# A one-core encoder kernel: attention outputs scaled by turned inverse sums instead of scaled probabilities, exponentials one pair ahead, dots moved behind attention

## The chip, the cores and the metric

The kernel runs on one core of one Trainium2 chip. The metric is the device time of one execution in microseconds. Before the change three runs took 2780.69, 2788.65 and 2793.71 us, so the median is 2788.65 us. Everything is float32.

## What is computed

One layer of a hybrid encoder is applied to two batches of 512 tokens of width 1024, with shared weights. Cut to what matters here:

```
h  = RMSNorm(x);  z = h @ W_in            # pool channels | q | k | v | two gates
A  = pooling mixer(pool channels)
s  = (q . k) * 64**-0.5                   # 8 query heads share 2 key/value heads, head size 64
pr = softmax(s, over 512 keys);  B = pr @ v
x += W_out( sigmoid(gate_pool) * (A @ W_pool_out) + sigmoid(gate_attn) * (B @ W_attn_out) )
# PEER: per token 8 heads x 16 experts = 128 experts out of 16384
a   = h2 . expert_u[idx]                  # 128 dot products of 1024 per token
x  += sum( gelu(a) * softmax gate * expert_v[idx] )
y   = RMSNorm(x)
```

The softmax subtracts the row's maximum, takes exponentials, and divides by their sum over the 512 keys.

## The kernel before

**Groups.** A batch has four tiles of 128 tokens. The mixer runs in three groups (`GROUP_OF`, L65): group 0 is tiles 0 and 1 of batch 0, group 1 its tiles 2 and 3, group 2 all four tiles of batch 1. A group goes through gates and pooling products, attention, eight steps of gate and attention products (`attn_out`), output products in chunks of 256 columns (`out`), the second norm, and the queries and keys of PEER. The order on each of the five engines is written out by hand in one block per engine; semaphores tie them together. Six PSUM banks go round over all jobs of TensorE in the order that `jobs_of` (L172) yields. A job waits until the bank of six jobs ago is freed.

**Attention.** A step is one tile, one pair of heads and one of its halves, so a tile has eight steps, or four pairs. For a pair TensorE does the scores of the next pair (L872, 128x512 into a bank each), the values of the pair before (L886, into `o_banks`), and then the transposes of this pair's probabilities (L703, four of 128x128 a step). VectorE takes each row's negative maximum (L1559). ScalarE takes the exponential with the sum in `prob_sum` (L1175). VectorE inverts the sum (L1566). The probabilities are then multiplied by it: by VectorE in group 0 (L1569), by ScalarE in groups 1 and 2 (L1191). TensorE turns them, and ScalarE moves the two turned banks to SBUF (L1048, into `gate_attn` or `keys_sb`) for the values. At the end of a tile ScalarE moves the outputs from an `o_bank` to `attnT` (L1180).

**Gathered rows.** From the first queries on, GpSimd gathers expert rows from DRAM one slot of 128 tokens at a time (L1429, 128 rows of 4 KB each, here called a row). The order is fixed: 128 rows of `expert_u` of tile (0,0), 128 of `expert_v`, the same for tile (0,1), then three more tiles. A row goes to one of twelve ring slots and may be asked for when the slot's last user is done. VectorE uses a `u` row by one dot product over 1024 columns (L1464, `dot(count)`), and frees the slot. The number of dots at each place of VectorE's program is written by hand:

```
            attention(2, 1)
            softmax(2)
            softmax(3)
            split_ids(0)
            dot(11)
            attn_out(2, (7, 7, 7, 7, 7, 6, 0, 0))
            zero_sums(1)
            turn_ids(2, 1)
            dot(4)
            out(2, (4, 4, 4, 4, 4, 4, 4))
            norm2(2)
```

The numbers in brackets are the dots behind each step. TensorE starts the output products only when all eight merged steps are there (`merged_ready`, L942). What is left of the 128 dots is done early in the queries of group 2; then ScalarE takes the gelu (L1275), VectorE weighs it by the gates (L1843), and TensorE turns the weights (L764). In group 1 the rows of the first tile are used likewise. The last stage, from about 1415 us on, streams all experts once for the three tiles that are done densely, and adds the remaining gathered tiles beside it.

## Time and profile before

| What | us |
|---|---|
| median of three runs | 2788.65 |
| profiled execution | 2784.83 |
| its span | 2783.0 |
| TensorE busy (matmuls) | 2589.6 (93%) |
| VectorE busy | 2035.8 (73%) |
| GpSimd busy | 1556.3 (56%) |
| ScalarE busy | 537.8 (19%) |

The mean granted TensorE clock is 0.972 of full speed. The gathers' queue moves 671.17 of 996.18 MB. The three attention stages lie at 149 to 182, 372 to 408 and 821 to 903 us.

In the rows below, PE is TensorE's matmuls, PEld its weight loads, DVE VectorE, ACT ScalarE, POOL GpSimd. A row of an engine in time has its start, how long it lasted in us, the engine, the source line, and in brackets the idle time just before it with what ended it. "x8" counts instructions as the profiler records them: a float32 matmul appears twice. "issue" and "remote" are idle times without a releaser that the profile knows.

### The profile page before, as it was taken

To read this page: it belongs to the slowest core of one execution; us is meant where nothing else is said; L and a number is where in the kernel's file an instruction comes from. 1 tells how busy PE (TensorE), PEld (TensorE's weight loads), DVE (VectorE), ACT (ScalarE), POOL (GpSimd) and SP (SyncE) were. 2 spreads that over 40 slices of the span, in tenths; PEclk is the share of its full clock that TensorE was granted. 3 is DMA by queue.
4 is the path that set the end of the run, shared out by engine and by line. 5 is a ranking of instruction groups with operands and counts; after the bars stand their busy time and mean duration, and the time that the engine had idled before them with its cause. 6 is when DMAs were issued, how large, how long until landed. Compare 5 with 4: busy or idle time off the path is not lost.

```text
span 2783.0 us, 30841 instructions
## 1 busy us (share of the span) xinstructions
PE 2589.6 (93%) x9957; PEld 1551.2 (56%) x9957; DVE 2035.8 (73%) x4558; ACT 537.8 (19%) x1206; POOL 1556.3 (56%) x1284
## 2 busy tenths in 40 slices
PE   7999989989997998998699999999999999999997
PEld 6867868875334475554554455455545455445553
DVE  1232977877348877788789988977777877877788
ACT  2141151211018014554510000100000000000101
POOL 0000155455665785444277786786777666766674
PEclk9999999989999999999799999999999999999998
DMA  6538789988997898999899999999999999999997
GB/s 239 184 120 299 282 310 406 405 320 312 395 374 254 324 411 319 336 350 333 296 362 413 413 412 413 391 408 413 413 412 413 413 413 413 415 412 413 413 404 285
DMA packets 305988, 996.18 MB, mean 358 GB/s; under 512 B 26432, under 2 KB 107200, under 8 KB 276672
## 3 DMA queue, kind: packets, MB, share of 16 engines
q0 software_dynamic: 184320, 671.17, 62.3%
q1 hardware_dynamic: 69664, 292.02, 26.9%
q10 hardware_dynamic: 51872, 31.46, 3.7%
q8 instruction: 54, 0.88, 0.1%
q14 instruction: 78, 0.64, 0.1%
HBM read 932.68 MB, written 61.87 MB: 357 GB/s over the span
## 4 chain that ended last, share of the span: by engine, by line
PE 34%; DMA 27%; DVE 19%; issue 12%; POOL 3%; ACT 3%; another core or an unknown queue 1%; DVEq 0%; ACTq 0%; POOLq 0%
PE bank L725 13%; DMA ring<-in_expert_v,idx 12%; PE bank L713 9%; DMA ring<-in_expert_u,idx 8%; DVE ring L1464 5%; DMA h<-in_expert_v,idx 3%; PE o_bank L745 3%; POOL ring L1429 2%; PE bank L784 2%; DVE region_b L1481 2%; PE bank L1011 2%; PE o_bank L1001 2%; DMA h<-in_expert_u,idx 1%; DMA region_c<-in_expert_u,idx 1%
## 5 line engine op out<-in xcount | busy, mean ns | idle before, releaser
L1429 POOL DMA_INDIRECT ring<-in_expert_u,idx x465 | 597.9, 1286 | 624.9 <-DVE idx L1772 292.6
L1011 PE MATMUL bank<-wslot,gate_attn 128*128 128x512 f32 x1536 | 690.0, 599 | 26.9 <-DVE gate_attn L1821 26.9
L1001 PE MATMUL o_bank<-region_a,wslot 128*128 128x384 f32 x2048 | 682.4, 487 | 0.0
L1429 POOL DMA_INDIRECT ring<-in_expert_v,idx x423 | 480.9, 1137 | 324.7 <-issue 134.6
L1001 PEld LDWEIGHTS o_bank<-region_a,wslot 128*128 128x128 f32 x2048 | 390.3, 191 | 297.9 <-issue 61.1
L1011 PEld LDWEIGHTS bank<-wslot,gate_attn 128*128 128x128 f32 x1536 | 293.4, 192 | 379.1 <-issue 314.3
L1464 DVE CUSTOM_DVE_ANT_0 ring<-ring,h 128x1024 f32<-128x1024 f32 x377 | 447.3, 1222 | 56.4 <-DMA ring<-in_expert_u,idx 48.6
L1481 DVE SCALAR_TENSOR_TENSOR region_b<-ring,dots,region_b 128x1024 f32<-128x1024 f32 x256 | 328.5, 1283 | 106.0 <-DMA ring<-in_expert_v,idx 78.5
L1331 ACT ACTIVATE gate_attn<-o_bank 128x384 f32<-128x384 f32 x128 | 62.7, 490 | 1241.8 <-PE o_bank L1001 1212.4
L725 PE MATMUL bank<-region_b,wslot 128*128 128x256 f32 (+1 forms) x768 | 232.3, 461 | 1.6 <-ACT region_b L1048 1.6
L725 PE MATMUL bank<-region_a,wslot 128*128 128x256 f32 (+1 forms) x768 | 226.3, 453 | 1.1 <-ACT region_a L1048 1.1
L725 PEld LDWEIGHTS bank<-region_b,wslot 128*128 128x128 f32 x768 | 148.2, 196 | 82.8 <-issue 66.8
L725 PEld LDWEIGHTS bank<-region_a,wslot 128*128 128x128 f32 x768 | 144.6, 190 | 79.4 <-issue 65.2
L1429 POOL DMA_INDIRECT h<-in_expert_v,idx x113 | 133.5, 1182 | 86.6 <-PE o_bank L745 42.1
L1429 POOL DMA_INDIRECT h<-in_expert_u,idx x89 | 117.0, 1315 | 71.8 <-DVE dots L1464 44.7
L1429 POOL DMA_INDIRECT region_c<-in_expert_v,idx x104 | 117.6, 1131 | 47.3 <-issue 36.1
L784 PE MATMUL bank<-consts 128*128 128x128 f32 x768 | 108.1, 295 | 32.9 <-DVEq L1890 22.6
L713 PE MATMUL bank<-wslot,region_b 128*128 128x256 f32 x576 | 128.6, 384 | 10.4 <-issue 6.9
L1464 DVE CUSTOM_DVE_ANT_0 ring<-ring,consts 128x1024 f32<-128x1024 f32 x88 | 105.3, 1222 | 42.8 <-DMA ring<-in_expert_u,idx 32.5
L713 PE MATMUL bank<-wslot,region_a 128*128 128x256 f32 x576 | 127.8, 386 | 6.4 <-DVE region_a L1598 5.1
L1429 POOL DMA_INDIRECT region_c<-in_expert_u,idx x86 | 109.1, 1269 | 42.2 <-issue 24.1
L784 PEld LDWEIGHTS bank<-consts 128*128 128x128 f32 x768 | 99.8, 206 | 51.1 <-DVEq L1890 28.8
(214 smaller groups left out, 2860.7 us busy)
## 6 DMA issues: line engine op xcount, KB each, us to landing
wslot<-in_expert_uT SPq DMA_DIRECT2D x64, 1024.0 KB
wslot<-in_expert_v SPq DMA_DIRECT2D x64, 1024.0 KB
wslot<-kept_weights SPq DMA_DIRECT2D x53, 1024.0 KB
kept_weights<-wslot SPq DMA_DIRECT2D x29, 1024.0 KB, 8.6
expert_weights<-region_p ACTq DMA_DIRECT2D x24, 1024.0 KB
wslot<-in_w_in SPq DMA_DIRECT2D x13, 1024.0 KB
region_p<-expert_weights SPq DMA_DIRECT2D x8, 1536.0 KB
region_s<-expert_weights SPq DMA_DIRECT2D x7, 1536.0 KB
```

Of the source, the lines that this page charges most:

```text
L713: ins = nc.tensor.matmul(bank[:, tt * CHUNK:(tt + 1) * CHUNK], lhs[:, k, t * P:(t + 1) * P], w[:, k, :], start=(k == 0), stop=(k == KD - 1))
L725: ins = nc.tensor.matmul(bank[:, 0:cols.stop - cols.start], w[:, k, col:col + P], rhs[:, k, cols], start=(k == 0), stop=(k == steps - 1))
L745: ins = nc.tensor.matmul(sums[half][q * QUAD_ROWS:(q + 1) * QUAD_ROWS, :], sum_ws[part][:, r % SUM_BUFS, q, QUAD_ROWS - 1 - r:2 * QUAD_ROW ...
L784: ins = nc.tensor.matmul(bank[:, r * P:(r + 1) * P], one_hot_i[:, at1, :], one_hot_j[:, at1, :], start=True, stop=True)
L1001: ins = nc.tensor.matmul(dense_in[q][:, 0:DENSE_T], u_cols[slot][:, k, :], mergeds[1][:, k, T - DENSE_T:T], start=(k == 0), stop=(k == KD ...
L1011: ins = nc.tensor.matmul(dense_out[2 * t + n][:], hidden[q][:, t * P:(t + 1) * P], v_cols[slot][:, n * 512:(n + 1) * 512], start=start, st ...
L1331: nc.scalar.activation(hidden[q], dense_in[q][:, 0:DENSE_T], ACT.Gelu).then_inc(col_moved, 1)
L1429: nc.gpsimd.indirect_dma_start(ring_row(n), None, expert_u if what == "u" else expert_v, bass.IndirectOffsetOnAxis(ap=ids, axis=0)).then_i ...
L1464: nc.vector.tensor_tensor_reduce(row, row, h2_late[k], 1.0, 0.0, ALU.mult, ALU.add, dots[:, DOTS_AT[k] + s:DOTS_AT[k] + s + 1]).then_inc(s ...
L1481: nc.vector.scalar_tensor_tensor(out=x, in0=ring_row(n), scalar=dots[:, DOTS_AT[k] + s:DOTS_AT[k] + s + 1], in1=x, op0=ALU.mult, op1=ALU.a ...
```

## The change

Probabilities are no longer divided by their sum. The exponentials are turned and multiplied with the values as they are, the eight sums of a tile are inverted at once, spread to 512 columns (64 for each head) in a part of `region_q`, turned by TensorE as a new job "inverse" (four transposes a tile), and VectorE multiplies the tile's outputs in `attnT` by them. ScalarE's loop takes the exponentials of the next pair before it moves the turned ones of this pair, and VectorE takes maxima two pairs ahead. A score bank is freed by the exponential instead of the reciprocal. Attention has one dot for each pair of heads instead of two, and the dots that are gone are put behind it.

```
@@ jobs_of @@
+        if i and i % HEADS == 0:
+            yield (g, "inverse", GROUP_OF[g][1][i // HEADS - 1]), None
         yield (g, "probsT", i), None
         yield (g, "probsT", i + 1), None
+    yield (g, "inverse", GROUP_OF[g][1][-1]), None
...
-        prob_sum = sb("prob_sum", [P, 4])
+        prob_sum = sb("prob_sum", [P, TT, HEADS])
+        inverses = region_q[:, TT * QKV_W + HEADS * HD:TT * QKV_W + 2 * HEADS * HD]
...
@@ TensorE @@
+                def turn_inverses(t):
+
+                    pe.wait_ge(inverse_ready, b * TT + t + 1)
+                    turned((g, "inverse", t), range(PAIRS), lambda j: inverses[:, j * P:(j + 1) * P])
+
                         values(m - 1)
+                    if m and 2 * m % HEADS == 0:
+                        turn_inverses(steps[2 * m - 1][0])
                     for i in (2 * m, 2 * m + 1):
-                        pe.wait_ge(probs_ready, STEPS_BEFORE[g] + i + 1)
+                        moved(pe, g, "s", i)
                         turned((g, "probsT", i), range(TT), lambda s: probs[b][:, i % 4, s * P:(s + 1) * P])
                 values(len(steps) // 2 - 1)
+                turn_inverses(steps[-1][0])
...
-                        for t in tiles[-2:]:
-                            pe.wait_ge(o_freed[t % 2], (b * TT + t) // 2 + 1)
+                        for t in tiles:
+                            moved(pe, g, "inverse", t)
...
@@ ScalarE @@
+                exp(0)
+                exp(1)
+                if g == FIRST_GROUP[1]:
+                    gate_exp(1)
                 for i in range(0, n, 2):
-                    exp(i)
-                    exp(i + 1)
-                    if i == 0 and g == FIRST_GROUP[1]:
-                        gate_exp(1)
-                    for ii in (i, i + 1):
-                        if g:
-                            moved(act, g, "s", ii)
-                            nc.scalar.activation(probs[b][:, ii % 4, :], probs[b][:, ii % 4, :], ACT.Identity,
-                                                 scale=prob_sum[:, ii % 4:ii % 4 + 1]).then_inc(probs_ready, 1)
+                    if i + 2 < n:
+                        exp(i + 2)
+                        exp(i + 3)
+                    if i % HEADS == 0 and i:
+                        outputs(GROUP_OF[g][1][i // HEADS - 1])
...
                     for ii in (i, i + 1):
                         move(probsT(ii), (g, "probsT", ii))
-                    if i % HEADS == 0 and i:
-                        outputs(GROUP_OF[g][1][i // HEADS - 1])
                 outputs(GROUP_OF[g][1][-1])
...
@@ VectorE @@
-            def invert_sum(g, i):
-                dve.wait_ge(exp_ready, STEPS_BEFORE[g] + i + 1)
-
-                total = prob_sum[:, i % 4:i % 4 + 1]
-                nc.vector.reciprocal(total, total).then_inc(frees(g, "s", i), 1)
-                if g == 0:
-                    moved(dve, g, "s", i)
-                    nc.vector.tensor_scalar(probs[0][:, i % 4, :], probs[0][:, i % 4, :], total,
-                                            None, ALU.mult).then_inc(probs_ready, 1)
+            def invert_sums(g, t):
+
+                i = GROUP_OF[g][1].index(t) * HEADS
+                for ii in range(i, i + HEADS):
+                    moved(dve, g, "s", ii)
+                link(nc.vector.reciprocal(prob_sum[:, t, :], prob_sum[:, t, :]))
+                nc.vector.tensor_copy(inverses.rearrange("p (a d) -> p a d", a=HEADS),
+                                      prob_sum[:, t, :].unsqueeze(2).to_broadcast([P, HEADS, HD])).then_inc(
+                                          inverse_ready, 1)
+
+            def scale_outputs(g, t):
+
+                n = GROUP_OF[g][0] * TT + t
+                dve.wait_ge(o_freed[t % 2], n // 2 + 1)
+                bank = filled(dve, g, "inverse", t)
+                x = attnT[:, :, t * P:(t + 1) * P]
+                nc.vector.tensor_tensor(x, x, bank[:].rearrange("p (j q) -> p j q", q=P),
+                                        ALU.mult).then_inc(frees(g, "inverse", t), 1)
 
             def attention(g, rows=0):
...
-                row_max(g, 0)
-                row_max(g, 1)
+                for i in range(4):
+                    row_max(g, i)
                 for i in range(0, n, 2):
-                    invert_sum(g, i)
-                    invert_sum(g, i + 1)
+                    done = GROUP_OF[g][1][i // HEADS - 1] if i and i % HEADS == 0 else None
+                    if done is not None:
+                        invert_sums(g, done)
...
                     dot(rows)
-                    if i + 2 < n:
-                        row_max(g, i + 2)
-                        row_max(g, i + 3)
-                    dot(rows)
+                    if i + 4 < n:
+                        row_max(g, i + 4)
+                        row_max(g, i + 5)
+                    if done is not None:
+                        scale_outputs(g, done)
+                invert_sums(g, GROUP_OF[g][1][-1])
+                scale_outputs(g, GROUP_OF[g][1][-1])
...
             attention(1, 1)
-            dot(6)
+            dot(10)
...
-            dot(11)
-            attn_out(2, (7, 7, 7, 7, 7, 6, 0, 0))
+            dot(12)
+            attn_out(2, (7, 7, 7, 7, 7, 7, 2, 0))
...
-            out(2, (4, 4, 4, 4, 4, 4, 4))
+            out(2, (5, 5, 5, 5, 5, 5, 5))
```

On ScalarE, group 1, from the first exponentials on, before (`region_s` holds probabilities, `gate_attn` and `keys_sb` the turned ones):

```order
L1175 ACTIVATE region_s,prob_sum<-bank,neg_max 128x512 x2
L1191 ACTIVATE region_s<-region_s,prob_sum 128x512 x2
L1048 ACTIVATE gate_attn<-bank 128x512 x2
L1175 ACTIVATE region_s,prob_sum<-bank,neg_max 128x512 x2
L1191 ACTIVATE region_s<-region_s,prob_sum 128x512 x2
L1048 ACTIVATE keys_sb<-bank 128x512 x2
L1175 ACTIVATE region_s,prob_sum<-bank,neg_max 128x512 x2
L1191 ACTIVATE region_s<-region_s,prob_sum 128x512 x2
L1048 ACTIVATE gate_attn<-bank 128x512 x2
```

and now:

```order
L1190 ACT_TABLE_LOAD
L1190 ACTIVATE region_s,prob_sum<-bank,neg_max 128x512 x4
L1062 ACTIVATE gate_attn<-bank 128x512 x2
L1190 ACTIVATE region_s,prob_sum<-bank,neg_max 128x512 x2
L1062 ACTIVATE keys_sb<-bank 128x512 x2
L1190 ACTIVATE region_s,prob_sum<-bank,neg_max 128x512 x2
L1062 ACTIVATE gate_attn<-bank 128x512 x2
L1190 ACTIVATE region_s,prob_sum<-bank,neg_max 128x512 x2
L1062 ACTIVATE keys_sb<-bank 128x512 x2
```

The scaling passes are gone, and four exponentials stand before the first moves.

On VectorE, group 2, inside attention, two pairs before:

```order
L1559 TENSOR_REDUCE neg_max<-bank 128x1 x2
L1464 ISA region_c,dots<-region_c,h 128x1024
L1464 ISA dots 128x1
L1566 RECIPROCAL prob_sum<-prob_sum 128x1 x2
L1464 ISA ring,dots<-ring,h 128x1024
L1464 ISA dots 128x1
L1559 TENSOR_REDUCE neg_max<-bank 128x1 x2
L1464 ISA ring,dots<-ring,h 128x1024
L1464 ISA dots 128x1
L1566 RECIPROCAL prob_sum<-prob_sum 128x1 x2
```

and now, at the end of a tile (L1581 and L1582 make the inverses, L1592 scales the outputs of the tile in `region_p`):

```order
L1573 TENSOR_REDUCE neg_max<-bank 128x1 x2
L1581 RECIPROCAL prob_sum<-prob_sum 128x8
L1582 COPY region_q<-prob_sum 128x512
L1478 ISA region_c,dots<-region_c,h 128x1024
L1478 ISA dots 128x1
L1573 TENSOR_REDUCE neg_max<-bank 128x1 x2
L1592 TENSOR_TENSOR region_p<-region_p,bank 128x4x128
L1478 ISA region_c,dots<-region_c,h 128x1024
L1478 ISA dots 128x1
L1573 TENSOR_REDUCE neg_max<-bank 128x1 x2
```

Each pair has one dot (two lines, ISA) instead of two and no reciprocal; a tile's end has three instructions more, and the copy stands behind the maxima of a pair.

On VectorE, group 2, from the last two steps of `attn_out` (L1595 and L1598) on, before:

```order
L1464 ISA ring,dots<-ring,h 128x1024
L1464 ISA dots 128x1
L1595 TENSOR_TENSOR gate_attn<-gate_attn,bank 128x512
L1598 TENSOR_TENSOR region_a<-region_a,gate_attn 128x512
L1595 TENSOR_TENSOR gate_attn<-gate_attn,bank 128x512
L1598 TENSOR_TENSOR region_a<-region_a,gate_attn 128x512
L1610 MEMSET gate_attn 128x1024
L1615 CAST idx<-bank 128x128
L1464 ISA ring,dots<-ring,h 128x1024
L1464 ISA dots 128x1
L1464 ISA ring,dots<-ring,h 128x1024
L1464 ISA dots 128x1
```

and now (the same lines are L1622 and L1625):

```order
L1622 TENSOR_TENSOR gate_attn<-gate_attn,bank 128x512
L1625 TENSOR_TENSOR region_a<-region_a,gate_attn 128x512
L1478 ISA ring,dots<-ring,h 128x1024
L1478 ISA dots 128x1
L1478 ISA ring,dots<-ring,h 128x1024
L1478 ISA dots 128x1
L1622 TENSOR_TENSOR gate_attn<-gate_attn,bank 128x512
L1625 TENSOR_TENSOR region_a<-region_a,gate_attn 128x512
L1637 MEMSET gate_attn 128x1024
L1642 CAST idx<-bank 128x128
L1478 ISA ring,dots<-ring,h 128x1024
L1478 ISA dots 128x1
```

Two dots stand between the last two steps, where there were none. Counted from the end of attention, 52 dots stood before the last step of `attn_out`, and 56 do now.

## Rows read from the trace of the kernel before

**Rows 1.** By stretch: length; PE, PEld, DVE, ACT, POOL busy; granted clock; DMA share; GB/s.
```profile
821.00:902.50 81.50, 62.05 (x482) 35.98 (x480) 63.66 (x135) 63.12 (x133) 42.75 (x41) 0.94 0.80 277
...
902.50:940.00 37.50, 37.50 (x90) 16.70 (x89) 33.96 (x64) 4.66 (x8) 27.86 (x17) 1.00 0.80 267
...
980.00:1000.00 20.00, 14.94 (x46) 10.18 (x45) 14.47 (x25) 2.87 (x7) 16.03 (x14) 0.83 1.02 413
...
1415.00:1700.00 285.00, 279.59 (x756) 143.53 (x757) 251.86 (x535) 18.77 (x33) 215.90 (x162) 1.00 1.02 412
```

**Rows 2.** TensorE in time, group 1: start, us, instruction, idle before and releaser.
```profile
388.84 1.27 PE L703 MATMUL bank<-ident,region_s 128*128 128x128 f32 x8 [0.55 <-ACT region_s L1191]
...
392.76 1.27 PE L703 MATMUL bank<-ident,region_s 128*128 128x128 f32 x8 [0.57 <-ACT region_s L1191]
```

**Rows 3.** TensorE in time, group 0: transposes, scores, values, two later transposes.
```profile
158.50 1.09 PE L703 MATMUL bank<-ident,region_s 128*128 128x128 f32 x8
...
159.52 1.13 PE L872 MATMUL bank<-region_c,region_p 64*128 64x512 f32 x4
...
160.58 1.09 PE L886 MATMUL o_bank<-keys_sb,region_c 128*64 128x128 f32 x16
...
165.12 1.32 PE L703 MATMUL bank<-ident,region_s 128*128 128x128 f32 x8
...
168.52 1.32 PE L703 MATMUL bank<-ident,region_s 128*128 128x128 f32 x8
```

**Rows 4.** ScalarE in time, group 1, one pair: exponential, scalings, moves.
```profile
386.74 0.68 ACT L1175 ACTIVATE region_s<-bank,neg_max 128x512 f32<-128x512 f32 x1
...
388.06 1.33 ACT L1191 ACTIVATE region_s<-region_s,prob_sum 128x512 f32<-128x512 f32 x2
...
389.54 1.21 ACT L1048 ACTIVATE keys_sb<-bank 128x512 f32<-128x512 f32 x2
```

**Rows 5.** First scores and maxima of group 1, engines in time.
```profile
371.78 1.99 PE L872 MATMUL bank<-region_c 64*128 64x512 f32 x8
...
372.94 1.29 DVE L1559 TENSOR_REDUCE neg_max<-bank 128x1 f32<-128x512 f32 x2 [0.63 <-PE bank L872]
```

**Rows 6.** ScalarE in time, group 2, the pause.
```profile
843.10 1.08 ACT L1048 ACTIVATE keys_sb<-bank 128x512 f32<-128x512 f32 x2 [5.89 <-remote]
```

**Rows 7.** TensorE in time, group 2, first and last transposes.
```profile
830.48 1.27 PE L703 MATMUL bank<-ident,consts 128*128 128x128 f32 x8 [2.58 <-ACT consts L1191]
...
899.45 1.27 PE L703 MATMUL bank<-ident,consts 128*128 128x128 f32 x8 [0.76 <-ACT consts L1191]
```

**Rows 8.** End of the attention products, group 2: VectorE's dots, TensorE's output products.
```profile
986.75 1.22 DVE L1464 CUSTOM_DVE_ANT_0 ring<-ring,h 128x1024 f32<-128x1024 f32 x1 [1.04 <-DMA ring<-in_expert_u,idx]
...
999.72 1.23 DVE L1464 CUSTOM_DVE_ANT_0 ring<-ring,h 128x1024 f32<-128x1024 f32 x1 [2.53 <-issue]
...
990.68 58.54 PE L713 MATMUL bank<-wslot,region_a 128*128 128x256 f32 x256 [5.06 <-DVE region_a L1598]
```

**Rows 9.** GpSimd in time: gathers of rows, group 2 after attention.
```profile
908.46 1.14 POOL L1429 DMA_INDIRECT ring<-in_expert_u,idx  x1 [5.07 <-DVE dots L1464]
...
940.52 0.93 POOL L1429 DMA_INDIRECT ring<-in_expert_u,idx  x1 [0.30 <-issue]
...
983.38 1.99 POOL L1429 DMA_INDIRECT ring<-in_expert_u,idx  x1 [0.30 <-issue]
```

**Rows 10.** VectorE in time, output step of group 2.
```profile
1028.54 0.69 DVE L1627 TENSOR_TENSOR region_b<-region_b,bank 128x512 f32<-128x512 f32 x1 [1.64 <-PE bank L713]
```

**Rows 11.** First queries of group 2: ScalarE's table for the gelu, VectorE's weighing.
```profile
1077.56 1.28 ACT L1275 ACT_TABLE_LOAD   x1
...
1079.20 0.29 DVE L1843 TENSOR_TENSOR dots<-dots,gate 128x128 f32<-128x128 f32 x1 [5.66 <-ACT dots L1275]
```

**Rows 12.** Group 1 after attention: VectorE's first product, TensorE's transposes of batch 1.
```profile
417.06 0.42 DVE L1595 TENSOR_TENSOR gate_attn<-gate_attn,bank 128x256 f32<-128x256 f32 x1 [3.39 <-PE bank L725]
...
558.00 6.29 PE L703 MATMUL bank<-ident,region_a 128*128 128x128 f32 x32 [3.69 <-DVE region_a L1496]
```

9 lines of the change are left out of this document (6 added, 3 removed).

## The prediction

> **What bounds the kernel now.** I read the busy times by stretch first, then each engine in order of time through the three attention stages, then VectorE, GpSimd and TensorE from the end of the last attention to the first queries. The three attentions are group 0 (two tiles, 149 to 182 us), group 1 (two tiles, 371.8 to 408) and group 2 (four tiles, 821 to 902.5). In the last, TensorE is busy 62.05 of 81.5 us and the DMA share is 0.80 [rows 1]: there the loop over pairs of heads sets the time. Behind it the picture turns: the share is 1.02 from 980 to 1000 and again in the long last stage from 1415 on [rows 1]. In that last stage the data set the time, so its length does not change, and a microsecond won or lost before it arrives at the end whole. The question is thus how much sooner the last stage starts.
>
> A pair in groups 1 and 2 takes 3.92 us (transposes at 388.84, the next at 392.76), and at each the transposes wait about 0.55 us for ScalarE's scaling [rows 2]. Without waits, as in group 0 at 158.50, TensorE needs 1.02 for eight transposes, 1.06 for the scores and about 1.08 for the values [rows 3]: 3.16 us. Later pairs of group 0 take 3.40 (165.12 to 168.52), 0.24 of it waiting. ScalarE does two exponentials in 1.32 us (386.74 to 388.06), two scalings in 1.48 (to 389.54) and two moves in 1.21 [rows 4]; that is all of 3.9.
>
> **Attention, part by part.** The scaling pass goes: 48 ScalarE passes of 1.33 us per pair [rows 4], and 16 on VectorE in group 0. ScalarE's pair becomes 1.32 + 1.21 = 2.53 us, under TensorE's 3.16. With exponentials a pair ahead, moves no longer stand behind them. VectorE's pair becomes two maxima, 1.29 together [rows 5], and one dot instead of two, 1.22 busy [rows 8] and 1.15 from start to start back to back, as neighbours overlap: some 2.5 us, also under 3.16. So TensorE bounds the pair.
>
> What is added, per tile: a reciprocal of 8 columns, a copy to 512 columns, and a product of 512 columns, for which I take the 0.69 us of the sum of the same size [rows 10]; four transposes, half of 1.02, so 0.5 us. The copy and the reciprocal together I take at 0.7; below 0.3 or above 1.4 would surprise me. They are queued behind the two maxima of the pair that TensorE has just scored, so at a tile's end inside a group the four transposes wait: in group 1 the first scores start at 371.78 and two maxima behind them end at 374.23 [rows 5], 2.45 later; then 0.7 and a handover make 3.4 us from the start of the scores, where TensorE is free after 1.06 + 1.08 = 2.1. I price this inner end at 1.3 + 0.5 = 1.8 us (0.5 to 2.5). The ScalarE output move (about 0.45 in the old loop) stays but is covered. Behind the waiting transposes stand the next probability transposes, and nothing of the gathers. At the last tile of a group only 0.5 is seen, because 14 us of gate products cover VectorE's part.
>
> - Group 0: 7 periods x 0.24 = 1.7 less 1.8 less 0.5, plus the old output move: about 0 (-1 to +1.5).
> - Group 1: 7 x 0.76 = 5.3, the first transposes 1.1 sooner (no 1.33 us scaling before them), less 1.4 for the inner end, less 0.5: 4.5 won (2 to 6.5).
> - Group 2: from the first transposes at 830.48 to the last at 899.45 are 69.0 us [rows 7]. New: 15 x 3.16 = 47.4, 3 x 1.8 = 5.4, and 2.2 at the start, where sums and softmax stand: 55.0. With 1.2 sooner at the front and 0.5 later at the end, 14.7 won. But before the move at 843.10 ScalarE stood for 5.89 us with a releaser that the profile does not know [rows 6], and TensorE behind it. Whether such a pause returns elsewhere decides 8.8 or 14.7; I take 12.
>
> Together 16.5 us won in attention (10 to 21).
>
> The Trainium skill, in "Runtime: NRT & Kernel Launch", section "Instruction fetch mechanics", has each engine stream its code in blocks through a DMA queue of its own and calls the cost mostly hidden. By it the pauses would not come back, and 14.7 would stand; the 5.89 us speak against "mostly hidden" if they are such a fetch, which no row here proves.
>
> **The dots that are moved.** Attention now does one dot a pair instead of two. In group 1 eight are moved; four are taken up in front of the first attention product (6 to 10), four at the very end of the row of 128. In group 2 sixteen are moved: 11 to 12 in front, 41 to 44 in the attention products, 28 to 35 in the output step, and 12 to 17 after the second norm. Each needs its gathered row, and only 12 rows fit ahead. At 902.5 all 12 are there in both kernels: at 908.46 GpSimd had waited 5.07 us for a free slot [rows 9]. So the k-th new row can be asked for only after the k-th dot, and the rows saved during attention cannot be fetched in advance.
>
> After attention the stream decides. The last attention product needed 52 dots before (11, five times 7, and 6); it needs 56 now (12, six times 7, and 2). In the trace the 52nd started at 986.75 after a wait for DMA, and TensorE began the output products at 990.68 after waiting 5.06. The 56th dot started only at 999.72 [rows 8], although its row had been asked for at 983.38 [rows 9]: 2 MB of residual and weights were in the same queues at a share of 1.02 [rows 1]. Before, these four dots lay beside the output products and cost nothing. Now 999.7 + 1.2 for the dot + 1.4 for the last product and sum = 1002.3: TensorE starts **11.6 us** later, counted from the end of attention. That is what takes the place of the gain. Bounds: 3.4 (four dots at 1.15 less cover, if all rows landed) and 14.
>
> An output step is 0.69 for the sum, 4 x 1.15 for dots and 1.64 idle, waiting for TensorE [rows 10]: 6.9 us, TensorE's pace. A fifth dot takes 1.15, so by VectorE it fits. The rows: 6.9 us at 413 GB/s [rows 1] are 2.85 MB, less half a chunk of weights and keys (0.59) 2.26 MB, or 4.3 rows of 0.52 a step, not 5; but the late start gives a few rows in hand; I take 1 us (0 to 13, below). After the second norm VectorE had done its 12 dots 5.66 us before 1079.20, at 1073.54, and ScalarE came to the gelu at 1077.56 [rows 11]; five more dots end at 1073.54 + 5.73 = 1079.3: 1.8 us later. So group 2 pays back 11.6 + 1 + 1.8 = 14.4 us.
>
> Group 1: ten dots instead of six, starting about 1 us after attention: the first attention product, which VectorE waited for 3.39 us at 417.06 [rows 12], is 4.8 late; the waits of the next steps take this up but for 1. Then the rows are late by about five at 1.28 us each (0.52 MB at 413 GB/s) in a stretch of full DMA, less what slack there is: 3.5 us at the first norm of the second batch, where TensorE already waits 3.69 for VectorE at 558.00 [rows 12]. I take 3.5 (1 to 7).
>
> **Sum.** 2784.8 (the profiled execution) - 16.5 + 14.4 + 3.5 = 2786.2 us. The median of the three runs is 2788.65, 3.8 above the profiled one, so this is 0.1% under the median: no change. I say 2786.
>
> **Rivals.**
> 1. *The rows are in time.* TensorE starts the output step only 3.4 later and group 1 pays 1. For it: DMA has a share of only 0.80 in 902.5 to 940 [rows 1], and VectorE's own time has room for every moved dot. Against it: the 999.72 row. Time: 2784.8 - 16.5 + 3.4 + 1.8 + 1 = 2774.5; with no returning pause 2771.5. Chance 0.25.
> 2. *Slower: GpSimd cannot issue 5 rows a step.* While dots run back to back an issue takes 1.99 + 0.30 = 2.29 us (983.38); beside an idle VectorE 0.93 + 0.30 = 1.23 (940.52) [rows 9]. With 5 dots, 5.7 us of a step yield 2.5 rows and the rest one each 1.23 us: a step of 8.8 us instead of 6.9. It decides once the 12 rows ahead are used up. Seven steps cost 13.3, and with ScalarE's pause back in attention 3.3 more: 2785.2 + 13.3 + 3.3 = 2802. Chance 0.18. Beside this: the Trainium skill, "GPSIMD Engine Reference", section "Key points", says that GpSimd shares its SBUF interfaces with VectorE and contends with instructions that have two SBUF inputs; a dot is one, and the two lengths of an issue agree. By that rule moving dots out of attention, where they are spread out, into rows of 12 and 7, is what slows the gathers.
> 3. *The change does not do what it says:* the pair stays at about 3.4, since values wait for moves that stand behind the exponentials of the next pair. For it: group 0's 3.40 without scaling on ScalarE. Against: there ScalarE idles. Then 23 periods win 0.24 less: 2786.2 + 5.5 = 2792. Chance 0.12.
>
> **How the numbers follow.** My forecast has 0.45. Half a percent, 14 us, is about what can be told from no change: faster is under 2774.7, slower over 2802.6. Faster: half of rival 1, and a tenth of the forecast, with some weight for payback that is smaller in both groups: 0.22. Slower: half of rival 2 and the tails of the others: 0.13. Same: 0.65. The range 2768 to 2803 takes in rival 1 without a pause and rival 2.
>
> **What would show it.** The pair at 3.1 to 3.2 us in all groups with TensorE dense; inner tile ends of 1.8; group 2's attention 65 to 72 us long. Then TensorE's wait before the output products at 14 to 18 us instead of 5.06, with VectorE in front of it waiting for gathered rows; that row settles forecast against rival 1. Output steps of 6.9 or of 8 to 9 us settle rival 2. If that wait stays under 8 us, the prediction is wrong and the kernel is faster.

## The result: 0.8% slower, where no change was forecast

The changed kernel took 2810.03 us (median of 8 runs) against 2789.24 (8 runs): the ratio is 1.0077 with an interval of 1.0057 to 1.0097, so 21 us slower. The forecast was 2786, its range ended at 2803.

First the profiled execution (2814.42 us, span 2812.6). Its stretches, in the columns of [rows 1]: group 1's attention, group 2's attention, from there to the output products, and the output products (here up to the last sum; to the norm's first transpose, as in all tables below, they take 70.3).

```profile
378.97:413.08 34.11, 27.98 (x233) 17.93 (x233) 21.45 (x38) 21.84 (x51) 7.69 (x8) 0.95 0.49 150
845.38:919.00 73.62, 59.67 (x498) 36.72 (x497) 45.49 (x81) 43.22 (x102) 25.99 (x27) 0.95 0.64 223
919.00:1006.59 87.59, 83.00 (x198) 36.80 (x197) 79.35 (x139) 8.94 (x18) 65.58 (x53) 0.99 0.90 344
1006.59:1071.70 65.11, 58.44 (x256) 50.64 (x256) 51.39 (x88) 6.36 (x28) 50.21 (x40) 0.92 1.03 411
```

TensorE in time. A pair (group 1), an inner tile end (inverses, then the second step's transposes), the last two pairs, and the first output product of group 2:

```profile
388.00 1.09 PE L709 MATMUL bank<-ident,region_s 128*128 128x128 f32 x8
391.10 1.09 PE L709 MATMUL bank<-ident,region_s 128*128 128x128 f32 x8
...
398.64 0.66 PE L709 MATMUL bank<-ident,region_q 128*128 128x128 f32 x4 [0.92 <-DVE region_q L1582]
...
403.29 0.63 PE L709 MATMUL bank<-ident,region_s 128*128 128x128 f32 x4 [0.45 <-DVE region_p L1592]
...
408.35 1.09 PE L892 MATMUL o_bank<-gate_attn,region_c 128*64 128x128 f32 x16 [1.32 <-ACT gate_attn L1062]
...
411.56 1.09 PE L892 MATMUL o_bank<-keys_sb,region_c 128*64 128x128 f32 x16 [1.10 <-ACT keys_sb L1062]
...
1006.59 33.62 PE L719 MATMUL bank<-wslot,region_a 128*128 128x256 f32 x141 [4.59 <-DVE region_a L1625]
```

The pair is 3.10 us, as forecast (before: 3.92, [rows 2]). An inner end costs 0.66 for the inverses, 0.92 and 0.45 of waiting, so a tile of four pairs takes 14.83 us (889.73 to 904.56 in group 2) where it took 16.16. At the group's end the values wait 1.32 and 1.10 for ScalarE's moves, which the forecast left out. They wait for moves in two more places of group 2: 0.27 once in each tile, and 1.30 and 1.47 at the first two pairs (the latter two in the third profile). The output products wait 4.59, against 5.06 in [rows 8] and the 14 to 18 forecast. By the forecast's own sign (a wait under 8 us) the kernel should then be faster, and it is slower. The row can't decide alone: the output step behind it is 6.5 us longer than before (70.3 against 63.8). And these two profiles differ in pauses that belong to neither program. GpSimd in the profile of the changed kernel, start and us of a gather's issue:

```profile
340.19 8.02 POOL L1443 DMA_INDIRECT ring<-in_expert_u,idx  x1 [38.49 <-DVE dots L1478]
...
594.62 8.01 POOL L1443 DMA_INDIRECT ring<-in_expert_u,idx  x1 [2.25 <-DVE dots L1478]
```

Two issues of 8.0 us stand in this execution and in none of the other seventeen profiles of this study (the longest elsewhere is one of 5.45 us, in attention_alone); the first starved the dots in front of group 1's attention and made it start 7 us late. ScalarE's pause of 5.89 us in [rows 6] is another matter. In the second profile of before it is gone, and group 2's attention takes 71.91 us, not 81.12. But it is not the chance of one execution, for the changed kernel has it too. ScalarE in its second profile, in front of the moves of the same pair of group 2:

```profile
842.73 1.09 ACT L1062 ACTIVATE keys_sb<-bank 128x512 f32<-128x512 f32 x2 [5.37 <-remote]
```

TensorE's values behind these moves wait 4.04 us in the first profile of before, 3.32 and 6.96 in the first two of the changed kernel, and at most 1.5 later. The kernels were timed in five rounds. In the six profiles of the first two rounds ScalarE is idle for over 4 us without a known releaser 18 to 24 times each, in the twelve of the last three rounds never. The changed kernel's attention of group 2 took 73.6 and 74.0 us in the early rounds, and 65.9 in all five later profiles of the same code; the old one 81.1 and (dots_alone) 73.8 early, and 71.9, 71.1 and 71.2 later. So the early rounds lengthen attention in both kernels, and a profile with these pauses must not be subtracted from one without. What they are is not known.

So the comparison is made with a second profile of before (2742.75 us) and a third of the changed kernel (2768.95), on one chip and in one round. TensorE at the first output product of group 2, before and changed:

```profile
957.32 2.86 PE L713 MATMUL bank<-wslot,region_a 128*128 128x256 f32 x12 [2.26 <-DVE region_a L1598]
```

```profile
977.94 22.25 PE L719 MATMUL bank<-wslot,region_a 128*128 128x256 f32 x91 [13.36 <-DVE region_a L1625]
```

The wait is 2.26 before and 13.36 now. In the changed kernel's second profile it was 16.42, in its fourth 10.10; why it was 4.59 in the first is not shown. What the wait spares, the output step takes: from the end of group 2's attention to the norm's first transpose the four profiles of the changed kernel have 157.9, 164.4, 163.2 and 160.1 us, the two of before 152.0 and 146.5. The stretches of the two, first before:

```profile
800.04:871.95 71.91, 58.54 (x481) 33.90 (x481) 63.07 (x134) 63.23 (x133) 44.25 (x39) 0.98 0.88 312
871.95:957.32 85.37, 83.11 (x199) 36.96 (x197) 73.50 (x130) 9.25 (x18) 65.99 (x49) 1.00 0.92 346
957.32:1018.38 61.06, 55.52 (x256) 48.62 (x256) 47.24 (x81) 7.63 (x34) 43.45 (x37) 0.97 1.03 411
```

```profile
815.72:881.58 65.86, 56.37 (x497) 35.07 (x497) 45.43 (x81) 42.89 (x102) 24.11 (x24) 1.00 0.68 239
881.58:977.94 96.36, 83.00 (x198) 36.80 (x196) 78.56 (x139) 8.94 (x18) 74.04 (x54) 0.95 0.89 333
977.94:1044.74 66.80, 57.87 (x256) 50.18 (x256) 55.32 (x95) 7.57 (x33) 51.18 (x40) 0.93 1.02 400
```

Group 2's attention is 6.0 us shorter and moves its data at a share of 0.68 instead of 0.88; the next stretch is 11.0 longer, the output products 5.7. The whole balance of the two executions, from the starts of the same instructions (us by which the changed kernel is behind, and what each stretch added):

| at | behind | added |
|---|---|---|
| group 0's first scores | 0.8 | |
| group 0's attention over | 2.2 | +1.4 |
| group 1's first scores | 2.0 | -0.2 |
| group 1's attention over | -1.1 | -3.2 |
| its output products over | 4.6 | +5.7 |
| first tile's gelu weighed | 12.1 | +7.5 |
| group 2's first scores | 15.7 | +3.6 |
| group 2's attention over | 9.6 | -6.0 |
| first output product | 20.6 | +11.0 |
| output products over | 26.4 | +5.7 |
| second tile's gelu weighed | 28.7 | +2.3 |
| end of the span | 26.3 | -2.4 |

Both are single draws: this one of before is 10 us under its kernel's median on that chip (2753.09), so some 10 of the 26 may be luck, and the timed kernels below decide on sizes.

### The profile page after: what moved, and what is told of

It reads as the page before. It is cut to its first block, busy times and chain, and to the rows that moved or that the text cites. A ratio compares the mean times of both kernels' runs of the same rounds, so it can differ in the third digit from the quotient of the medians.

```text
span 2812.6 us, 30850 instructions
## 1 busy us (share of the span) xinstructions
PE 2597.5 (92%) x9989; PEld 1557.4 (55%) x9989; DVE 2032.3 (72%) x4502; ACT 506.3 (18%) x1158; POOL 1557.3 (55%) x1284
## 4 chain that ended last, share of the span: by engine, by line
DMA 29%; PE 27%; DVE 25%; issue 12%; POOL 5%; ACT 1%; another core or an unknown queue 1%; DVEq 0%; POOLq 0%; ACTq 0%; SPq 0%
DMA ring<-in_expert_v,idx 9%; DMA ring<-in_expert_u,idx 9%; PE bank L731 8%; PE bank L719 7%; DVE ring L1478 7%; DMA region_c<-in_expert_v,idx 3%; POOL ring L1443 3%; DMA h<-in_expert_v,idx 3%; DVE region_b L1495 3%; PE o_bank L751 3%; PE bank L790 2%; DMA h<-in_expert_u,idx 2%; PE bank L709 1%; DVE h L1478 1%; DMA region_c<-in_expert_u,idx 1%
## 5 line engine op out<-in xcount | busy, mean ns | idle before, releaser
L1478 DVE CUSTOM_DVE_ANT_0 ring<-ring,h 128x1024 f32<-128x1024 f32 x377 | 448.2, 1228 | 75.6 <-DMA ring<-in_expert_u,idx 63.2
L790 PE MATMUL bank<-consts 128*128 128x128 f32 x768 | 109.3, 297 | 37.7 <-DVEq L1917 31.2
L1478 DVE CUSTOM_DVE_ANT_0 ring<-ring,consts 128x1024 f32<-128x1024 f32 x88 | 105.3, 1223 | 45.1 <-DMA ring<-in_expert_u,idx 37.7
```

The lines of the kernel that those rows point to most:

```text
L790: ins = nc.tensor.matmul(bank[:, r * P:(r + 1) * P], one_hot_i[:, at1, :], one_hot_j[:, at1, :], start=True, stop=True)
L1478: nc.vector.tensor_tensor_reduce(row, row, h2_late[k], 1.0, 0.0, ALU.mult, ALU.add, dots[:, DOTS_AT[k] + s:DOTS_AT[k] + s + 1]).then_inc(s ...
```

## The experiments

All are ratios to the kernel before, run beside them in the same round and on the same chip. Its level differs from round to round, on one chip too: 2789 us in the round of the result, 2775, 2753 and 2753 in three rounds on one chip, 2754 in the last on another. A comparison of two rows of different rounds is therefore weaker than its intervals say. Round two has attention_alone, dots_alone and group2_dots_back; three the late_inverse kernels with one and two dots, half_dots and half_rows; four fifty_two_rows and late_inverse_more_dots; five the kernels with group1 in their names, group2_dots_moved and changed_fourth.

| kernel | ratio | interval |
|---|---|---|
| changed | 1.0077 | 1.0057 to 1.0097 |
| changed_fourth (the same, another chip) | 1.0063 | 1.0047 to 1.0079 |
| attention_alone | 1.0046 | 1.0027 to 1.0066 |
| dots_alone | 1.0088 | 1.0058 to 1.0117 |
| group2_dots_back | 1.0057 | 1.0034 to 1.0079 |
| group1_dots_moved | 1.0017 | 1.0004 to 1.0030 |
| group2_dots_moved | 1.0045 | 1.0032 to 1.0057 |
| group1_dots_back | 1.0028 | 1.0017 to 1.0040 |
| half_dots | 1.0030 | 1.0016 to 1.0044 |
| half_rows | 1.0076 | 1.0047 to 1.0104 |
| fifty_two_rows | 1.0082 | 1.0061 to 1.0103 |
| late_inverse_one_dot | 1.0035 | 1.0019 to 1.0051 |
| late_inverse_two_dots | 0.9973 | 0.9957 to 0.9989 |
| late_inverse_more_dots | 0.9981 | 0.9969 to 0.9993 |

And what their profiles show in us: attention of groups 0, 1 and 2 (first scores to the first product behind it), from group 2's attention to its first output product, and those products with the norm (to its first transpose).

| kernel | g0 | g1 | g2 | to outputs | outputs |
|---|---|---|---|---|---|
| before, first | 33.3 | 36.3 | 81.1 | 88.2 | 63.8 |
| before, second | 32.2 | 37.0 | 71.9 | 85.4 | 61.1 |
| changed, first | 33.0 | 34.1 | 73.6 | 87.6 | 70.3 |
| changed, second | 33.6 | 33.2 | 74.0 | 99.4 | 65.0 |
| changed, third | 33.6 | 33.8 | 65.9 | 96.4 | 66.8 |
| changed, fourth | 33.0 | 33.8 | 65.9 | 93.1 | 67.0 |
| attention_alone | 33.8 | 37.7 | 77.7 | 87.4 | 62.5 |
| dots_alone | 33.6 | 37.0 | 73.8 | 93.0 | 69.9 |
| group2_dots_back | 33.0 | 33.2 | 84.1 | 87.5 | 62.3 |
| group1_dots_moved | 32.2 | 36.9 | 71.1 | 89.1 | 62.6 |
| group2_dots_moved | 32.2 | 37.0 | 71.2 | 93.8 | 67.2 |
| group1_dots_back | 33.8 | 38.7 | 65.9 | 88.8 | 72.3 |
| half_dots | 33.6 | 33.8 | 65.3 | 84.1 | 69.7 |
| half_rows | 33.0 | 33.8 | 65.9 | 91.5 | 71.9 |
| fifty_two_rows | 33.0 | 33.8 | 65.9 | 84.9 | 73.1 |
| late_inverse_one_dot | 31.7 | 32.6 | 62.1 | 84.9 | 74.3 |
| late_inverse_two_dots | 32.4 | 34.5 | 67.7 | 87.4 | 62.2 |
| late_inverse_more_dots | 31.7 | 34.6 | 77.2 | 85.3 | 60.8 |

**Attention or dots.** In attention_alone the changed kernel gets back the second dot and the old counts:

```diff
                         row_max(g, i + 5)
+                    dot(rows)
-            dot(10)
+            dot(6)
-            dot(12)
-            attn_out(2, (7, 7, 7, 7, 7, 7, 2, 0))
+            dot(11)
+            attn_out(2, (7, 7, 7, 7, 7, 6, 0, 0))
-            out(2, (5, 5, 5, 5, 5, 5, 5))
+            out(2, (4, 4, 4, 4, 4, 4, 4))
```

> The new attention (no scaling pass, inverses turned, exponentials and maxima ahead) with the old dots: two in each pair of heads, and the old counts behind. Theory A (the dots that were moved cost the time, because each takes a row of 0.52 MB out of a stretch with DMA to spare and puts it where DMA is full, 1.27 us each at 413 GB/s; 24 rows are 30 us): all rows stand where they stood, so this kernel is not slower than before. VectorE now sets the pair: two maxima 1.29 and two dots 2.30 are 3.6 us against 3.92, so group 1 wins 7 x 0.3 less the inner end and group 2 some 15 x 0.3 less three inner ends: 0 to 8 us in all, 2781 to 2789. Theory B (the new attention is what costs, by its inner ends, its waits for the inverses or by code that lies elsewhere): clearly slower than before, 2800 or more. The wait of TensorE before the output products of group 1 should be 1 us again and that of group 2 about 5; the output steps 6.9.

In dots_alone the kernel before loses the second `dot(rows)` of a pair and gets the new counts, the same edit the other way round.

> The old attention, with one dot in each pair of heads instead of two, and the dots that are gone behind it, in the same numbers as in the changed kernel. Theory A (moved rows cost 1.27 us each in full DMA, 24 of them): attention keeps ScalarE's pace of 3.92 us and gives nothing back, so 20 to 30 us slower than before, 2809 to 2819, and at least as slow as the changed kernel. Theory B (the new attention costs): within 5 us of before. Output steps of group 2 of 7.8 us on average instead of 6.9 in theory A.

In group2_dots_back the second dot comes back for group 2 only (`if g in (2,): dot(rows)`), with the old counts behind it.

> The changed kernel with two dots a pair again in group 2 alone, and the old counts behind group 2; group 1 has one dot a pair and the moved dots as in the changed kernel. It splits the loss by group. Theory A: 16 of the 24 rows go back to where DMA has room, and the pair of group 2 is 3.6 us instead of 3.1: 20 us won by the rows, 7 lost by the slower pairs, so 13 us faster than the changed kernel, about 2797, 8 us above before. Rival: the loss is all in group 1 and before group 2 (in the profile of the changed kernel the first scores of group 2 are 24.0 us late already): then this is 2805 to 2815.

> The changed kernel once more, for a second profile. In the first one two gathers of GpSimd took 8.0 us each (340.19 and 594.62) where none of before took over 3. If they belong to the code, they stand here at the same instructions; if they are chance, they don't, and the first scores of group 1 start some 7 us sooner than 378.97. Time 2802 to 2825 as in its eight runs.

The moved dots alone cost 0.88%, 24 us: theory A's sign and size. But the new attention alone costs too, 0.46% or 13 us, where I expected none: both theories were half right. TensorE in attention_alone, two inner ends of group 2:

```profile
879.62 0.55 PE L709 MATMUL bank<-ident,region_q 128*128 128x128 f32 x3 [1.86 <-DVE region_q L1582]
...
885.41 0.63 PE L709 MATMUL bank<-ident,consts 128*128 128x128 f32 x4 [1.59 <-DVE region_p L1592]
...
897.23 0.66 PE L709 MATMUL bank<-ident,region_q 128*128 128x128 f32 x4 [1.72 <-DVE region_q L1582]
...
903.03 0.63 PE L709 MATMUL bank<-ident,consts 128*128 128x128 f32 x4 [1.59 <-DVE region_p L1592]
```

The inverses wait 1.7 to 1.9 for VectorE's copy, which stands behind a dot and two maxima, and the transposes behind them 1.6 for the bank that `scale_outputs` frees. A tile takes 17.6 us, 1.4 more than before. group2_dots_back lies between, as theory A has it, though 8 us dearer than it said; its tile of group 2 takes the same 17.6 us. But its 16 us above before are also the lower end of what the rival said, and its interval takes in the changed kernel's ratio, so this kernel alone does not split the loss by group. The second profile of the changed kernel has neither 8-us issue and starts its first scores of group 1 at 371.33: these two issues were chance.

**The inner tile end.** The two late_inverse kernels turn the inverses behind the next pair's transposes, and VectorE makes them ahead of its second dot:

```diff
-        if i and i % HEADS == 0:
-            yield (g, "inverse", ...), None
         yield (g, "probsT", i), None
         yield (g, "probsT", i + 1), None
+        if i and i % HEADS == 0:
+            yield (g, "inverse", ...), None
...
                     if done is not None:
                         scale_outputs(g, done)
+                    if i + 2 < n and (i + 2) % HEADS == 0:
+                        invert_sums(g, GROUP_OF[g][1][i // HEADS])
+                    dot(rows)        # two dots only
```

> The new attention with two dots a pair and the old counts behind it (as in attention_alone), and the inverse's job moved: TensorE turns the inverses behind the next pair's transposes instead of in front of them, and VectorE makes them in front of its second dot. attention_alone showed a tile of 17.6 us against 16.16 before, with TensorE waiting 1.7 to 1.9 for the inverses and 1.6 for the scaled outputs' bank at each tile's end, and was 0.46% slower than before. Theory C (what makes the new attention slower with the same rows is these two waits at the inner ends): they go, VectorE sets the tile with 8 maxima, 8 dots and 1.2 us for the inverses, 15.2 us; against attention_alone six tiles x 2.4 are 14 us won, so 0.1% faster than before (-0.3 to +0.1%). Rival (code in another place, or rows that come late whatever attention does): within 0.15% of attention_alone, 0.3 to 0.6% slower than before.

> The changed kernel (one dot a pair) with the same late inverse. A tile of attention should take 13.1 us instead of 14.83, so group 2's attention is 5 to 7 us shorter than the changed kernel's and group 1's 2. Theory A (rows set the time behind attention: each comes only every 1.6 to 1.7 us, and 24 of them were pushed there): group 2's shorter attention comes back as a longer wait before the output products, of 20 us instead of 16.4, and the time stays within 3 us of the changed kernel, 0.65 to 0.85% above before. Rival (shorter attention counts in full): 7 to 9 us faster than the changed kernel, 0.45 to 0.5% above before.

TensorE in late_inverse_two_dots, the inverses of two tiles of group 2, with no wait:

```profile
838.50 0.66 PE L709 MATMUL bank<-ident,region_q 128*128 128x128 f32 x4
...
853.68 0.66 PE L709 MATMUL bank<-ident,region_q 128*128 128x128 f32 x4
```

A tile takes 15.18 us (expected 15.2), and the kernel is 0.27% faster than before: theory C holds, and this is the version that beats both. (attention_alone was timed in an early round, so how much of the way from 1.0046 to 0.9973 the inverses account for is less sure; the three attentions of the two profiles differ by 14.6 us, of 20.) With one dot (tile 13.53, expected 13.1) it is 0.35% slower than before, 0.28 to 0.42% (8 to 12 us) better than the changed kernel, which was timed in other rounds: nearer to the rival's 7 to 9 us than to theory A's 3, which the intervals don't quite exclude. Its group 2 has the longest output step of all, 74.3 us, so part of the shorter attention may be given back there.

**What sets the pace of the rows.** The issue times depend on VectorE. GpSimd in the changed kernel's second profile, in attention (a slot's user has just finished, and no dot runs beside the issue) and behind it, where dots run back to back:

```profile
852.86 0.94 POOL L1443 DMA_INDIRECT h<-in_expert_u,idx  x1 [5.84 <-DVE dots L1478]
...
910.67 1.99 POOL L1443 DMA_INDIRECT ring<-in_expert_u,idx  x1 [0.30 <-issue]
912.96 1.99 POOL L1443 DMA_INDIRECT ring<-in_expert_u,idx  x1 [0.30 <-issue]
915.25 1.99 POOL L1443 DMA_INDIRECT ring<-in_expert_u,idx  x1 [0.31 <-issue]
```

Counted over 300 to 1400 us of the first profile of before: of 312 issues with no dot beside them 4 took over 1.6 us (mean 1.00); of 91 that dots cover for nine tenths or more, 43 did (mean 1.47); of the 115 between, 13 (mean 1.19). The Trainium skill, "GPSIMD Engine Reference", section "Key points" (GpSimd shares SBUF interfaces with VectorE and contends with two-input instructions), fits these numbers. In half_dots the 128 dots of tile (0,1) take half the columns (`row[:, 0:512]`), in half_rows its gathers bring half the bytes (`expert_u` seen as rows of 512, width 512).

> The changed kernel, where the 128 dots of tile (0,1) take 512 of the 1024 columns: that half of the products is left out. The rows are gathered whole. In the traces a gather's issue takes 0.94 us where VectorE does no dot, and 1.5 to 1.6 on average, over half of them near 2.0, where dots cover it. Theory G (behind attention GpSimd is the bound: it issues without a pause, 1.4 + 0.3 us a row, and dots on VectorE lengthen the issues): long issues all but go, a row takes 1.3 instead of 1.7, and the stretch from group 2's attention to the output products shrinks from 99 (second profile of the changed kernel) to about 88 us; 10 to 20 us faster than the changed kernel. Theory D (the DMA queues are the bound there): the stretch stays within 3 us and the time within 5.

> The changed kernel, where the 128 gathered rows of tile (0,1) are 512 columns wide instead of 1024, taken from the first half of the table: half of their bytes is left out, and the products are not the reference's. As many gathers are issued and the dots are as long as before. Theory D (DMA bound behind attention, 1.27 us for a row of 0.52 MB): 55 rows less 0.64 us each are 35 us less in that stretch, until VectorE or TensorE bounds it: the wait before the output products falls from 16.4 to about 5, the time by 15 us or more. Theory G (GpSimd's issues bound it): the stretch stays at 95 us or more, since as many issues stand behind as many dots, and the time falls by under 6 us.

The two stretches behind group 2's attention, half_rows first, then half_dots:

```profile
879.54:971.06 91.52, 83.00 (x198) 36.80 (x196) 78.35 (x139) 8.93 (x18) 70.43 (x50) 0.98 0.65 217
971.06:1042.94 71.88, 56.91 (x256) 49.57 (x256) 54.76 (x95) 7.56 (x33) 59.69 (x41) 0.90 0.70 229
```

```profile
882.90:967.04 84.14, 83.00 (x199) 36.80 (x197) 49.36 (x139) 7.75 (x17) 53.13 (x55) 1.00 0.93 366
967.04:1036.71 69.67, 55.52 (x256) 48.56 (x257) 35.82 (x95) 8.75 (x35) 39.34 (x40) 0.93 1.02 410
```

With half the bytes the DMA share falls from 0.89 and 1.02 to 0.65 and 0.70, and nothing is won: 91.5 and 71.9 us, in sum 163.4 as in the changed kernel (163.2 and 160.1), and the timed kernel is no faster. GpSimd issues 91 rows there at a mean of 1.43 us, with 0.30 between two; that is 157 of the 163 us. With half the dots the issues take 0.97, GpSimd is busy for 53 us instead of 74, the way to the output products is 84.1 (TensorE's own 83.0), and the kernel is 0.33 to 0.47% (9 to 13 us; 10 to 20 expected) faster than the changed one, timed in other rounds. So up to the output products GpSimd is the bound, not DMA. In the output step half_dots moves 410 GB/s at a share of 1.02 and stays at 69.7: there both limits seem equally near, since lifting either alone gained nothing. (half_dots also frees VectorE's own time, so it is no pure test of the issues; that half_rows wins nothing needs no such caution.)

fifty_two_rows asks whether my wait for the 56th row is where the time goes, with the old 52 dots before the last attention product and the four others behind the norm:

```diff
-            dot(12)
-            attn_out(2, (7, 7, 7, 7, 7, 7, 2, 0))
+            dot(11)
+            attn_out(2, (7, 7, 7, 7, 7, 6, 0, 0))
```

> The changed kernel, but the last attention product of group 2 needs 52 dots again and not 56; the four dots go behind the second norm (28 are to be done there, then, instead of 24 less what is spent). Forecast's step (the wait for the 56th row, 11.6 us, is what eats the gain, and dots behind the norm are cheap): TensorE starts the output products 5 to 7 us sooner and pays back four dots, 4.6 us at most: faster than the changed kernel by 2 to 6 us, 0.55 to 0.7% above before. Theory G (what counts is the number of rows that GpSimd must still issue behind attention, at 1.4 to 1.7 us each, wherever VectorE uses them): the rows are the same 94, so the output steps come late instead and the time stays within 3 us of the changed kernel, 0.65 to 0.9% above before.

TensorE starts the output products with a wait of 1.90 instead of 10 to 13, the output step grows from 67 to 73.1, and the time is that of the changed kernel (1.0082). Theory G holds: what counts is the number of rows still to be issued, wherever VectorE uses them, and the wait is only where the missing rows show.

In late_inverse_more_dots group 2's attention has three dots in every other pair (`dot(rows + (g == 2 and i % 4 == 0))`) and the attention products `(6, 6, 6, 5, 5, 5, 0, 0)`.

> late_inverse_two_dots with eight dots more in group 2's attention (three instead of two in every other pair) and eight fewer in the attention products behind it, 44 before the last instead of 52. VectorE sets the pair there, so a dot costs 1.15 us in attention: 9.2 us longer. Theory G: eight rows fewer for GpSimd behind attention, at 1.7 us each 13.6 us shorter there, so 4 us faster than late_inverse_two_dots, 0.35 to 0.5% faster than before. Rival (TensorE, not the rows, sets the 87.4 us between attention and the output products: it works 83.0 of them already, and waits 4.35): nothing comes back but those 4 us at most, and the kernel is 5 us slower than late_inverse_two_dots, 0.0 to 0.15% faster than before.

Attention is 9.5 us longer, the two stretches behind it only 3.5 shorter; the ratio is 0.9981, within the interval of two dots. The rival is nearer: the way to the output products is 85.3 us, of which TensorE works 83.0, so a row less has little left to give.

**Second profiles and the groups.**

> The kernel before once more, for a second profile beside a third one of the changed kernel on the same chip. In its first trace ScalarE paused for 5.89 us in group 2's attention (before 843.10) and VectorE for 11.55 before 824.89. If both are chance they are gone, group 2's attention takes 75.2 us instead of 81.1, and the new attention's lead shrinks from 7.3 to some 9.9 less its own pauses; if they belong to the program, they stand at the same places. The stretch from group 2's attention to the output products should be 88 us in either case, the output step 6.9.

> The changed kernel a third time, on the same chip as the second profile of before. Stretch by stretch against it: group 1's attention 3 us shorter, its output products 4 us late, group 2's attention 8 to 10 us shorter when neither pauses, 10 us or more from there to the output products against 88, and output steps of 7.8 against 6.9; in sum 10 to 25 us longer than before.

Both came out beyond what I expected: the second profile of before is shorter (group 2's attention 71.9 for 75.2, 85.4 behind it for 88), so the new attention leads by 6.0 us and not by 8 to 10, and the whole difference is 26.3 us.

The last four leave or put back the dots of one group only, in the kernel before (`if g != 1: dot(rows)` with `dot(10)`; `if g != 2:` with the new counts of group 2) and in the changed one.

> The kernel before, with only the eight dots of group 1's attention moved as in the change (one a pair, four of them in front of the attention products, four at the end of the tile's 128). The forecast priced group 1's payback at 3.5 us. The second profile of before and the third of the changed kernel, on one chip, show 14.4 us between the end of group 1's attention and the weighing of the first tile: 1.7 before the output products, 2.9 more in them, 7.5 at the end of the 128 dots, where nothing stands beside them, and the rest between. Ledger: 10 to 16 us slower than before, 0.35 to 0.6%, though the old attention hides nothing and gives nothing. Forecast's size: 3 to 5 us, 0.1 to 0.2%.

> The kernel before, with only the sixteen dots of group 2's attention moved as in the change. The forecast priced this at 14.4 us; the ledger from the two profiles on one chip is 11.0 until the output products, 5.7 in them and 2.3 behind, 19 us. With dots_alone at 0.88% (24 us) for both groups, group 2's share should be 10 to 19 us, 0.35 to 0.7% slower than before. If group 1 costs the 14 of the ledger, this is nearer to 10.

> The changed kernel with two dots a pair again in group 1, and the old six in front of its attention products; group 2 as in the changed kernel. Group 1's attention then takes 37.7 us as in attention_alone instead of 33.8, 3.9 longer, and 14.4 of payback goes: 10 us faster than the changed kernel beside it (0.2 to 0.5%). By the forecast's sizes (attention 3.9 longer, payback 3.5 gone) it would be the same as the changed kernel.

> The changed kernel beside the three others on the same chip, so that they can be compared with it directly: 0.6 to 0.95% above before. Its profile tells once more whether gathers of 8.0 us come again: seen twice in the first profile and in none of eleven others; all theories expect none, or one by chance.

Group 1's eight rows cost 4.7 us (1.1 to 8.3), the forecast's size and not the 14.4 of two single profiles; group 2's sixteen 12.4 (8.8 to 15.7), about the forecast's 14.4 and below the 19 of the balance. With the changed kernel beside it group1_dots_back is 0.35% or 9.6 us faster, as expected: in the new attention group 1's rows seem dearer, and why is not settled.

## Why the prediction was wrong

No change was forecast, and the kernel lost 0.8%. The step that failed is what attention gains, group 2's above all: 12 us were taken, 5 to 7.5 are there. The second is the output step, priced at 1 us. The exchange that the forecast saw (shorter attention against rows that come late) is the right one, and its price for the moved rows is about right; only the gain was half.

1. *The pair of 3.16*: right, 3.10, and TensorE dense in it. Rival 3's mechanism, values that wait for moves, is there only in part: 0.27 us once in each tile of group 2, and 1.30 and 1.47 at its start.
2. *The inner end of 1.8*: 14.83 less 4 x 3.10 is 2.4. Small in the forecast, but with the inverses turned one step later the kernel is 0.28 to 0.42% faster (late_inverse_one_dot).
3. *Group 0 gains nothing*: it lies between 0.3 us won and 1.4 lost. The values of the last two pairs wait 1.32 and 1.10 for the moves; I had counted no end of a group but 0.5 for the inverses.
4. *Group 2's attention gains 12*: this step failed. From the first transposes to the last the forecast has 55.0 us; the third profile has 56.7, so the new attention was foreseen well. The old was not: its 69.0 of [rows 7] hold the pause of [rows 6] and are 63.2 in the second profile of before. I subtracted an attention without pauses from one with. I asked whether the pause "returns elsewhere" and took mostly no. In the early rounds it did return, in the changed kernel too: there the first transposes to the last are 64.1 and 64.7, and the whole attention 73.6 and 74.0 against 81.1, 7.1 to 7.5 won. In the later rounds neither has it: 71.9 (71.1, 71.2) against 65.9, 5.2 to 6.0 won. With group 1 (2.2 to 3.2, 4.5 forecast) and group 0 attention gains 8 to 10 us, not 16.5.
5. *The output products start 11.6 later*: right in mechanism, not sure in size. It is 11.0 and 7.7 us in the third and fourth profiles against the second of before, but about 4 in the fourth against group1_dots_moved, which has the old code there (89.1 us) and was profiled in the same round, and nothing in the first profile. Only the sum with the output step is steady: 157.9 to 164.4 us in the four profiles of the changed kernel, 146.5 to 152.0 in the two of before and group1_dots_moved. The sign that was to settle it (a wait under 8 us, then a faster kernel) was no good sign: fifty_two_rows has a wait of 1.90 and the full loss. The price was attached to DMA by the row of 999.72; half_rows shows that it is GpSimd's issues.
6. *The output steps cost 1 us in all*: too small. They cost 5.7 in the third profile against the second of before, 6.5 in the first against the first, 4.4 in the fourth against group1_dots_moved. My own numbers gave 4.3 rows in 6.9 us; a fifth is 0.52 MB more, so a step of 3.2 MB at 413 GB/s is 7.8 us, and seven of them 6 us. I let "a few rows in hand" cancel that. VectorE in the first profile of the changed kernel has the sums at

```profile
1016.79 0.69 DVE L1654 TENSOR_TENSOR region_b<-region_b,bank 128x512 f32<-128x512 f32 x1 [4.06 <-issue]
...
1023.62 0.69 DVE L1654 TENSOR_TENSOR region_b<-region_b,bank 128x512 f32<-128x512 f32 x1 [0.39 <-PE bank L719]
...
1032.69 0.68 DVE L1654 TENSOR_TENSOR region_b<-region_b,bank 128x512 f32<-128x512 f32 x1
...
1071.66 0.68 DVE L1654 TENSOR_TENSOR region_b<-region_b,bank 128x512 f32<-128x512 f32 x1
```

   seven steps in 54.87 us, 7.84 each. The rows in hand are real but few: in the third profile the first four steps still take 6.8 to 6.9 us, the last three 7.6 to 9.1. Rival 2 (chance 0.18) had the mechanism, a step of 8.8, and with 2802 the nearest time.
7. *After the second norm 1.8*: 2.3. *Group 1's payback 3.5*: 4.7 timed.

Payback as forecast is 17.9; timed with the old attention it is 17 (groups 1 and 2 added) or 24 (dots_alone). With 8 us gained, 2784.8 comes to 2794 or 2801; the ratios (1.0063 and 1.0077 times 2784.8) give 2802 to 2806. So the missing gain explains 8 of the 16 to 20 us that the forecast was short, and dearer rows up to 7. What is left, 1 to 12 us, is not explained; the intervals are 4 to 6 us to either side, and rows may be dearer behind the new attention, as group1_dots_back hints. (Of the 24 us between 2786 and 2810.03, 4 more are only that the profiled execution, from which I added up, lay under the median of 2789.24.) A hidden part is the second dot: the new attention as built, with two dots, is itself slower than the old, so the change could win only by giving up dots, and each one given up cost 0.6 to 1.0 us behind attention in the timed kernels.

## What to carry to other kernels

Before pricing a stretch, profile the kernel twice, the second time in another round: two profiles of one round can both hold pauses that belong to no program, and a gap without a known releaser is no gain to be had. Work that paces a stream (a row per dot) is not moved for free out of a stretch where the stream has room, wherever it is put; count what the stream must still bring behind that point, and at what pace. And a short serial job between two pipelined ones (the inverses) belongs one step late, behind work that needs no answer from it.

## What was not expected of the hardware

The issue of a gather on GpSimd takes 0.94 us beside an idle VectorE and up to 1.99 beside dots, and this, not the DMA queues, paced the rows up to the output products: halving their bytes won nothing. Two issues took 8.0 us in one profile of eighteen. VectorE's pause of 11.55 us and ScalarE's of 5.89 in the first profile of before were gone in the second, but ScalarE's stood in the changed kernel's second profile too (5.37 us): ScalarE has such idle times in all six profiles of the two early rounds and in none of the twelve later ones, whatever the kernel. The Trainium skill, "Runtime: NRT & Kernel Launch", section "Instruction fetch mechanics", calls the cost of fetching code mostly hidden. No run shows that the pauses were fetches: the instruction queue q8 has the same 54 packets in both profiles of before, 1.01 and 1.00 us each on average.
